# Search stage of a transformer block: the up weights' high parts copied right behind each Gelu, and the sums over gathered pairs moved apart from the next dots, with ScalarE's and GpSimd's orders changed to match

## The chip, the cores and the metric

The kernel runs on one core of a Trainium2 chip. The metric is the device time of one execution in microseconds (us). TensorE (PE) multiplies matrices, VectorE (DVE), ScalarE (ACT) and GpSimd (POOL) work on tiles, SyncE (SP) issues most of the transfers. Each engine runs its own instructions strictly in the order in which they were written; engines wait for each other by semaphores.

## The reference, cut to what matters

The whole reference is two transformer blocks over 512 tokens of width 1024. The change lies in the feed-forward part of the first block, a retrieval among 16384 single-neuron experts:

```python
q = einsum('bsd,de->bse', h, w_q).reshape(B, S, 8, 256)
s1 = einsum('bshd,hnd->bshn', q[..., :128], keys1)      # 128 keys a half
s2 = einsum('bshd,hnd->bshn', q[..., 128:], keys2)
v1, i1 = top_k(s1, 16); v2, i2 = top_k(s2, 16)
cand = v1[..., :, None] + v2[..., None, :]               # 256 candidates
vals, c = top_k(cand, 16)
expert = i1[c // 16] * 128 + i2[c % 16]
gate = softmax(vals)
u = u_tab[expert]; v = v_tab[expert]
out = einsum('te,ted->td', gate * gelu(einsum('td,ted->te', h, u)), v)
```

Three of the four blocks of 128 tokens are computed densely: all 16384 experts' `h . u` (the "up" products) go through the Gelu, are multiplied by a matrix of gates that is zero for experts that were not chosen, and then by all of `v_tab`. The fourth block of 128 tokens is computed by gathering: for each of its 128 chosen (head, rank) pairs a token's row of `u` and `v` is fetched by an indirect transfer.

## The kernel before, in words

**Stages.** The kernel is written out per engine, stage by stage, with no scheduler: the order in the source is the order of execution. The stage around the change is the search stage (`pe_route`, `act_route`, `dve_route`, `pool_route`, `sp_route`), about 946 to 1380 us in the profile. After it come the stage that builds the gates (`*_gates`, to about 1608 us) and the dense down stage (`*_experts`, to about 2300 us).

**Rounds.** The search stage has eight rounds, c = 0 to 7, one for each search head. In a round TensorE multiplies the queries of head c+1 (two halves f, 24 matmuls each with three passes for high and low parts), then eight up tiles n = 8c to 8c+7 (`pe_up`, 24 matmuls with 384 columns each), with the scores of head c+1 after the fourth (`pe_scores`). There are no queries and scores in round 7.

**Up tiles.** Tile n needs its weights in two parts. `sp_u` loads them to `ur` (three buffers), `act_u_hi` (L1629, ScalarE) copies the high part to `uhl`, `u_lo` (L1635, in this stage on GpSimd) subtracts it to get the low part, `pe_up` multiplies, and `act_up` (L1659) takes the Gelu out of the bank. `uhl` has three buffers, so the high part of tile n waits for the end of product n-3. Below, "hi(n)" and "lo(n)" are these two steps. The output banks form a ring of four.

**Search on VectorE.** `dve_top16` runs twice in a round: over the keys' scores ("key search", L1889 to L1901 with 128 columns), and over the 256 candidates ("candidate search", the same lines with 256). GpSimd builds the candidates (L1968) after the key search. Then follow the split of the indices (L1925 to L1928), two one-hot tiles (L1931) which GpSimd multiplies by the indices (L1980), and the subtraction of the maximum (L1932, step `gmax`). ScalarE takes the Exp (L1870, after a load of its function table, L1868), VectorE divides by the sum (L1937 to L1941), reduces the two GpSimd products (L1945) and writes the expert numbers (L1948 to L1952, the last is a cast to integers, step `idx`).

**Gathered pairs.** There are 64 pairs t, each of two gathers of 128 rows with 8 KB (u and v behind each other). In each round from the second on, three pairs pass. `pool_gather` (L1689) issues pair t; it waits for the sums of pair t-2, since `gs` has room for two pairs. `dve_dots` (L1700) multiplies the u halves with the tokens; `act_tick` (L1726) takes the Gelu; `dve_sums` (L1707, L1713) adds the v halves to the sum, which stands in a bank. A `dve_tick(t)` is `dve_dots(t)` followed by `dve_sums(t-1)`.

**Other engines.** GpSimd also splits the query weights (`split_lo`, L240, two a round). SyncE issues in a round the eight loads of `ur`, the stores of the Gelu's results, and the loads of query weights and keys; its load for tile n+5 stands behind the store of tile n and waits for lo(n+2).

Of the kernel before, what the change touches and what calls it, by code (L numbers as in the profile page):

```python
# [192 lines left out]
def build(nc, a):  # L193
# [1429 lines left out]
    def act_u_hi(e, n):  # L1623
        T, A, V, G = UP
        if n < P:
            e.wait_ge(*u_land[n % 3].of(n))
            if n >= 3:
                e.wait_ge(*T.of("up", n - 3))
            e.activation(uhl[n % 3][:, 0, :], ur[:, n % 3, :], ACT.Copy).then_inc(*A.up("hi", n))  # L1629
# [19 lines left out]

    def act_up(e, R, n):  # L1650
        T, A, V, G = UP
        act_u_hi(e, n + 2)
        to = ag[n % 3] if n < NE else agd[turn[n] % 3]
        if n >= NE:
            e.wait_ge(*DN[2].of("w", turn[n] - 3))
        elif n >= 3:
            e.wait_ge(*ag_saved[n % 3].of(n - 3))
        e.wait_ge(*T.of("up", n))
        e.activation(to[:, :], R.bank("up", n)[:, 0:DT], ACT.Gelu).then_inc(*R.out(A, "up", n))  # L1659

    def sp_up(e, n):
        T, A, V, G = UP
# [59 lines left out]
    def act_tick(e, t):  # L1722
        T, A, V, G = GA
        if t < NB:
            e.wait_ge(*V.of("dot", 2 * t + 1))
            e.activation(ga[:, 2 * t:2 * t + 2], dot[:, 2 * t:2 * t + 2], ACT.Gelu).then_inc(*A.up("ga", t))  # L1726
# [4 lines left out]
    R5 = Ring(banks[0:4], after=R4x)  # L1731
# [104 lines left out]
    def act_scores(e, c):  # L1836
        T, A, V, G = Q
        for half in range(2):
            e.wait_ge(*T.of("s", c, half))
            if c >= 2:  # L1840
                e.wait_ge(*V.of("k4", c - 2, 7))
            e.activation(SC[c % 2][:, 4 * half:4 * half + 4, :], in4(R5.bank("s", c, half)),
                         ACT.Copy).then_inc(*R5.out(A, "s", c, half))

    def act_route(e):
        T, A, V, G = Q
        all_done(e, *MG)
        split_hi(e, W2, 0)
        act_u_hi(e, 0)
        act_queries(e, 0)  # L1850
        split_hi(e, W2, 1)
        act_u_hi(e, 1)
        e.activation(sump, x1[:, 3, :], ACT.Copy).then_inc(*GA[1].up("out"))
        act_scores(e, 0)
        e.wait_ge(*V.of("h"))
        e.activation(h2r[:, :], h2p, ACT.Copy).then_inc(*GA[1].up("h"))
        for c in range(8):
            if c < 7:
                act_queries(e, c + 1)
                split_hi(e, W2, 2 * c + 2)  # L1860
                split_hi(e, W2, 2 * c + 3)
            act_up(e, R5, 8 * c)
            act_up(e, R5, 8 * c + 1)
            if c:
                act_tick(e, 3 * c - 3)
            act_up(e, R5, 8 * c + 2)
            act_up(e, R5, 8 * c + 3)
            e.preload_act_table_set(LN_SET)  # L1868
            e.wait_ge(*V.of("gmax", c))
            e.activation(e16[:, 2, :, c, :], e16[:, 2, :, c, :], ACT.Exp).then_inc(*A.up("gexp", c))  # L1870
            if c < 7:
                act_scores(e, c + 1)
            if c:
                act_tick(e, 3 * c - 2)
            act_up(e, R5, 8 * c + 4)
            act_up(e, R5, 8 * c + 5)
            if c:
                act_tick(e, 3 * c - 1)
            act_up(e, R5, 8 * c + 6)
            act_up(e, R5, 8 * c + 7)  # L1880
        for tb in range(3):
            e.wait_ge(*T.of("eT", tb))
            e.activation(eT[:, :, blk(tb)], R5.bank("eT", tb)[:, 0:3 * P].rearrange("p (a c) -> p a c", a=3),
                         ACT.Copy).then_inc(*R5.out(A, "eT", tb))
# [19 lines left out]
    def dve_route(e):  # L1904
        T, A, V, G = Q
        all_done(e, *MG)
        split_lo(e, W2, 0)
        split_lo(e, W2, 1)
        e.wait_ge(*h_land.of("h"))
        e.scalar_tensor_tensor(out=h2p, in0=x1[:, 3, :], scalar=small[:, 7:8], in1=h2r[:, :], op0=ALU.mult,  # L1910
                               op1=ALU.mult).then_inc(*V.up("h"))
        for c in range(8):
            k = c % 2
            e.wait_ge(*A.of("s", c, 1))
            dve_top16(e, V, 8, SC[k], S2, v16[k], i16[k], "k", c)
            if c:
                e.wait_ge(*G.of("oh", c - 1, 1))
            e.wait_ge(*V.of("k4", c, 7))
            e.tensor_copy(if16[:, :, :], i16[k][:, :, :]).then_inc(*V.up("if", c))
            if c:  # L1920
                dve_tick(e, 3 * c - 3)
            e.wait_ge(*G.of("cand", c))
            dve_top16(e, V, NT, cand, cand2, vv, ii, "c", c)
            e.wait_ge(*V.of("c4", c, NT - 1))
            e.tensor_scalar(cc[:, 0, :, :], ii[:, :, :], 4, None, ALU.logical_shift_right).then_inc(*V.up("hi", c))  # L1925
            e.tensor_scalar(cc[:, 1, :, :], ii[:, :, :], 15, None, ALU.bitwise_and).then_inc(*V.up("lo", c))
            e.wait_ge(*V.of("lo", c))
            e.tensor_copy(cf[:, :, :, :], cc[:, :, :, :]).then_inc(*V.up("cf", c))  # L1928
            e.wait_ge(*V.of("cf", c))
            for i in range(2):  # L1930
                e.tensor_tensor(oh4[i], by16(cf[:, i, :, :]), iota16, ALU.is_equal).then_inc(*V.up("oh", c, i))  # L1931
            e.tensor_tensor(e16[:, 2, :, c, :], vv[:, :, :], vv[:, :, 0:1].broadcast_to([P, NT, 16]),  # L1932
                            ALU.subtract).then_inc(*V.up("gmax", c))
            if c:
                dve_tick(e, 3 * c - 2)
            e.wait_ge(*A.of("gexp", c))
            e.tensor_reduce(sm4[:, :], e16[:, 2, :, c, :], AX.X, ALU.add).then_inc(*V.up("gsum", c))  # L1937
            e.wait_ge(*V.of("gsum", c))
            e.reciprocal(sm4[:, :], sm4[:, :]).then_inc(*V.up("ginv", c))
            e.wait_ge(*V.of("ginv", c))  # L1940
            e.tensor_tensor(e16[:, 2, :, c, :], e16[:, 2, :, c, :],  # L1941
                            sm4[:, :].unsqueeze(2).broadcast_to([P, NT, 16]), ALU.mult).then_inc(*V.up("gate", c))
            for i in range(2):
                e.wait_ge(*G.of("oh", c, i))
                e.tensor_reduce(e16[:, i, :, c, :], oh4[i], AX.X, ALU.add).then_inc(*(V.up("e", c) if i else V.up("e0", c)))  # L1945
            e.wait_ge(*V.of("e", c))
            s16 = slice(16 * c, 16 * c + 16)
            e.scalar_tensor_tensor(out=idxf[:, :], in0=e16[:, 0, 3, c, :], scalar=float(P), in1=e16[:, 1, 3, c, :],  # L1948
                                   op0=ALU.mult, op1=ALU.add).then_inc(*V.up("idxf", c))
            e.tensor_copy(gg16[:, s16], e16[:, 2, 3, c, :]).then_inc(*V.up("gg", c))  # L1950
            e.wait_ge(*V.of("gg", c))
            e.tensor_copy(idx[:, s16], idxf[:, :]).then_inc(*V.up("idx", c))  # L1952
            if c:
                dve_tick(e, 3 * c - 1)

    def pool_route(e):
        T, A, V, G = Q
        all_done(e, *MG)
        u_lo(e, 0)
        u_lo(e, 1)  # L1960
        for c in range(8):
            k = c % 2
            lo = lambda n: u_lo(e, 8 * c + n)
            lo(2)
            if c:
                e.wait_ge(*V.of("e0", c - 1))
            e.wait_ge(*V.of("k4", c, 7))
            e.tensor_tensor(cand.rearrange("p h (i j) -> p h i j", i=16), by16(v16[k][:, 0:4, :]),  # L1968
                            of16(v16[k][:, 4:8, :]), ALU.add).then_inc(*G.up("cand", c))
            if c < 7:  # L1970
                split_lo(e, W2, 2 * c + 2)
                split_lo(e, W2, 2 * c + 3)
            lo(3)
            if c >= 2:
                pool_gather(e, 3 * c - 2)
            lo(4)
            lo(5)
            for i in range(2):
                e.wait_ge(*V.of("oh", c, i))
                e.tensor_tensor(oh4[i], oh4[i], of16(if16[:, 4 * i:4 * i + 4, :]),  # L1980
                                ALU.mult).then_inc(*G.up("oh", c, i))
            lo(6)
            if c:
                pool_gather(e, 3 * c - 1)
            lo(7)
            lo(8)
            if c:
                pool_gather(e, 3 * c)
            else:
                pool_gather(e, 0)  # L1990
                pool_gather(e, 1)
            lo(9)
# [1283 lines left out]
```

## Time and profile before

| what | value |
|---|---|
| time, median of 3 runs | 3006.16 us (3005.68 to 3009.01) |
| the profiled execution's own time | 3007.56 us |
| its span | 3005.8 us |
| PE / DVE / ACT / POOL busy, share of the span | 93% / 66% / 38% / 18% |
| granted TensorE clock, mean | 0.97 |
| search stage | 946 to 1380 us |

The span is what the profiler sees from the first to the last instruction; the execution's own time is 1.8 us longer. Shares over the whole span hide that stages have different limits; the rows below look at single stages. A row of a timeline gives start, length, engine, line, operation, output and inputs, and in brackets how long the engine had been idle before it and what ended that. "x2" joins neighbours. A line is one of the kernel before, whose numbers the changed kernel moves by a few (L1659 becomes L1658, L1968 becomes L1975, L1980 becomes L1989, L1868 and L1870 become L1874 and L1876).

### The profile page before, as it was taken

To read this page: it belongs to the slowest core of one execution; us is meant where nothing else is said; L and a number is where in the kernel's file an instruction comes from. 1 tells how busy PE (TensorE), PEld (TensorE's weight loads), DVE (VectorE), ACT (ScalarE), POOL (GpSimd) and SP (SyncE) were. 2 spreads that over 40 slices of the span, in tenths; PEclk is the share of its full clock that TensorE was granted. 3 is DMA by queue.
4 is the path that set the end of the run, shared out by engine and by line. 5 is a ranking of instruction groups with operands and counts; after the bars stand their busy time and mean duration, and the time that the engine had idled before them with its cause. 6 is when DMAs were issued, how large, how long until landed. Compare 5 with 4: busy or idle time off the path is not lost.

```text
span 3005.8 us, 36696 instructions
## 1 busy us (share of the span) xinstructions
PE 2787.5 (93%) x14045; PEld 2364.5 (79%) x14045; DVE 1972.8 (66%) x3643; ACT 1140.9 (38%) x1678; POOL 543.3 (18%) x390
## 2 busy tenths in 40 slices
PE   8999999999998998988997999999997987899997
PEld 6787878887777888887996888888886556688876
DVE  3335665665555789899995887887886485444434
ACT  5445144223224333336884222222223444322222
POOL 0111221120002767663111111111110011000000
PEclk9999999999999999998998999999998999999999
DMA  4112100005552666576888788888882200222220
GB/s 155 50 50 98 57 29 29 29 29 196 210 203 86 227 243 249 215 265 238 323 311 319 283 302 308 292 292 293 292 291 86 79 29 2 98 92 98 96 98 28
DMA packets 141358, 501.17 MB, mean 167 GB/s; under 512 B 13401, under 2 KB 67073, under 8 KB 111617
## 3 DMA queue, kind: packets, MB, share of 16 engines
q1 hardware_dynamic: 122752, 364.60, 34.5%
q0 software_dynamic: 18432, 134.23, 11.3%
q8 instruction: 113, 1.85, 0.3%
q14 instruction: 61, 0.49, 0.1%
HBM read 450.53 MB, written 48.25 MB: 166 GB/s over the span
## 4 chain that ended last, share of the span: by engine, by line
PE 62%; DVE 23%; DMA 7%; ACT 4%; issue 3%; POOL 1%; SPq 0%; DVEq 0%; ACTq 0%; POOLq 0%
PE bank L244 16%; PE bank L245 16%; PE bank L246 16%; DMA gs<-in_uv_dram,idx 4%; DVE HA L2058 3%; DVE bank L1713 2%; DVE gs L1700 2%; DVE xn L1508 1%; PE bank L2658 1%; PE bank L1090 1%; PE bank L1080 1%; PE bank L713 1%; PE bank L1096 1%; DMA w_raw<-in_w_in_dram 1%; DVE uhl L1635 1%
## 5 line engine op out<-in xcount | busy, mean ns | idle before, releaser
L244 PE MATMUL bank<-HH,uhl 128*128 128x384 f32 x1024 | 358.3, 350 | 45.3 <-POOL uhl L1635 41.4
L245 PE MATMUL bank<-HL,uhl 128*128 128x384 f32 x1024 | 352.7, 344 | 0.0
L246 PE MATMUL bank<-HH,uhl 128*128 128x384 f32 x1024 | 352.3, 344 | 0.0
L244 PE MATMUL bank<-vhl,awhl 128*128 128x512 f32 x768 | 300.4, 391 | 6.8 <-DVE awhl L2291 6.8
L246 PE MATMUL bank<-vhl,awhl 128*128 128x512 f32 x768 | 300.3, 391 | 0.0
L245 PE MATMUL bank<-vhl,awhl 128*128 128x512 f32 x768 | 300.3, 391 | 0.0
L1689 POOL DMA_INDIRECT gs<-in_uv_dram,idx x128 | 161.2, 1259 | 753.6 <-DVE x L1713 497.0
L2242 ACT ACTIVATE vhl<-vraw 128x1024 fp32r<-128x1024 f32 x128 | 135.8, 1061 | 419.2 <-PE bank L246 253.4
L244 PEld LDWEIGHTS bank<-HH,uhl 128*128 128x128 f32 x1024 | 198.8, 194 | 52.6 <-issue 36.5
L1635 POOL TENSOR_TENSOR uhl<-ur,uhl 128x1024 fp32r<-128x1024 f32 x66 | 159.0, 2418 | 421.2 <-ACT uhl L1629 420.8
L2247 DVE TENSOR_TENSOR vhl<-vraw,vhl 128x1024 fp32r<-128x1024 f32 x128 | 156.5, 1223 | 104.0 <-ACT vhl L2242 103.9
L244 PE MATMUL bank<-HH,whl 128*128 128x512 f32 x528 | 217.3, 412 | 5.2 <-DVE whl L240 3.9
L240 DVE TENSOR_TENSOR whl<-w_raw,whl 128x2048 fp32r<-128x2048 f32 x49 | 113.5, 2316 | 161.5 <-ACT whl L234 161.5
L245 PE MATMUL bank<-HL,whl 128*128 128x512 f32 x528 | 210.7, 399 | 0.0
L246 PE MATMUL bank<-HH,whl 128*128 128x512 f32 x528 | 210.5, 399 | 0.0
L245 PEld LDWEIGHTS bank<-HL,uhl 128*128 128x128 f32 x1024 | 199.0, 194 | 1.7
L246 PEld LDWEIGHTS bank<-HH,uhl 128*128 128x128 f32 x1024 | 198.2, 194 | 0.0
L240 DVE TENSOR_TENSOR wfhl<-wf_raw,wfhl 128x2048 fp32r<-128x2048 f32 x37 | 84.8, 2292 | 155.4 <-ACT wfhl L234 155.4
L244 PEld LDWEIGHTS bank<-vhl,awhl 128*128 128x128 f32 x768 | 144.9, 189 | 36.6 <-DVE awhl L2291 4.4
L246 PEld LDWEIGHTS bank<-vhl,awhl 128*128 128x128 f32 x768 | 145.0, 189 | 30.4
L245 PEld LDWEIGHTS bank<-vhl,awhl 128*128 128x128 f32 x768 | 144.9, 189 | 29.1
L244 PE MATMUL bank<-HH,wfhl 128*128 128x512 f32 x352 | 139.6, 397 | 0.0
(420 smaller groups left out, 6233.6 us busy)
## 6 DMA issues: line engine op xcount, KB each, us to landing
ur<-in_peer_u_dram SPq DMA_DIRECT2D x128, 512.0 KB, 5.9
vraw<-in_peer_v_dram SPq DMA_DIRECT2D x128, 512.0 KB, 4.5
w_raw<-in_w_in_dram SPq DMA_DIRECT2D x36, 1024.0 KB, 4.9
xn<-in_ada_rows_dram SPq DMA_DIRECT2D x48, 512.0 KB, 4.7
g_scratch<-stg SPq DMA_DIRECT2D x12, 2048.0 KB, 11.0
gti<-g_scratch SPq DMA_DIRECT2D x16, 1536.0 KB, 10.0
wf_raw<-in_f_w_in_dram SPq DMA_DIRECT2D x22, 1024.0 KB, 4.8
act_scratch<-ag SPq DMA_DIRECT2D x96, 192.0 KB, 4.2
```

Of the source, the lines that this page charges most:

```text
L240: e.tensor_tensor(lo, W.tile(k), r32(hi), ALU.subtract).then_inc(*W.low(k).up(k))
L244: e.matmul(out, l[0], r[0], start=start, stop=False)
L245: e.matmul(out, l[0], r[1], start=False, stop=False)
L246: return e.matmul(out, l[1], r[0], start=False, stop=stop)
L713: i = e.matmul(b[:, (j - s) * P:wid[s]], const("tri_ge") if j == s else ones, L[:, off[j]:off[j] + wid[j]], start=j == s, stop=j == NT - 1 ...
L1635: e.tensor_tensor(uhl[n % 3][:, 1, :], ur[:, n % 3, :], r32(uhl[n % 3][:, 0, :]), ALU.subtract).then_inc(*u_low(n).up("lo", n))
L1689: e.indirect_dma_start(gs[:, n % 4, :], None, a["uv"], bass.IndirectOffsetOnAxis(ap=idx[:, n:n + 1], axis=0)).then_inc(*gs_land[n % 4].up(n))
L1700: e.scalar_tensor_tensor(out=u, in0=u, scalar=1.0, in1=h, op0=ALU.mult, op1=ALU.mult, accum_out=dot[:, n:n + 1]).then_inc(*V.up("dot", n))
L1713: e.scalar_tensor_tensor(out=x, in0=gs[:, n % 4, D:2 * D], scalar=ga[:, n:n + 1], in1=x, op0=ALU.mult, op1=ALU.add).then_inc(*(V.up("ax", ...
L2058: n = e.tensor_scalar(HA[k][:, i, :], iota, eT[:, 0, tok + i:tok + i + 1], eT[:, 2, tok + i:tok + i + 1], ALU.is_equal, ALU.mult)
L2242: e.activation(vhl[j % 3][:, 0, :], vraw[:, j % 2, :], ACT.Copy).then_inc(*A.up("v", j))
L2247: e.tensor_tensor(vhl[j % 3][:, 1, :], vraw[:, j % 2, :], r32(vhl[j % 3][:, 0, :]), ALU.subtract).then_inc(*V.up("v", j))
```

## The change

The number of instructions on each engine stays the same, and so does what they compute. Four things are written in another order.

1. `act_up(n)` issued hi(n+2) ahead of the Gelu of tile n; now it issues hi(n+3) behind it. As hi(n+2) used to follow the Gelu of n-1 with only the round's other work between them, the change is that this other work (queries, Exp, scores, ticks) now comes after the copy. It holds in the later stages too, which use the same function. hi(2) is issued once ahead of the loop.
2. VectorE's sums of a pair no longer stand right behind the next pair's dots: each stands halfway between its own pair's dots and the next.
3. ScalarE copies the scores of head c+1 before the Exp of round c, takes one more Gelu (tile 8c+4) before that Exp, and moves the third tick of a round behind its last Gelu.
4. GpSimd issues its gathers earlier or later to match, and splits its two one-hot products around a lo.

```diff
     def act_up(e, R, n):
         T, A, V, G = UP
-        act_u_hi(e, n + 2)
         to = ag[n % 3] if n < NE else agd[turn[n] % 3]
...
         e.activation(to[:, :], R.bank("up", n)[:, 0:DT], ACT.Gelu).then_inc(*R.out(A, "up", n))
+        act_u_hi(e, n + 3)
...
         for c in range(8):
+            if c > 1:
+                act_tick(e, 3 * c - 4)
             if c < 7:
                 act_queries(e, c + 1)
...
             act_up(e, R5, 8 * c + 2)
             act_up(e, R5, 8 * c + 3)
+            if c < 7:
+                act_scores(e, c + 1)
+            act_up(e, R5, 8 * c + 4)
             e.preload_act_table_set(LN_SET)
             e.wait_ge(*V.of("gmax", c))
             e.activation(e16[:, 2, :, c, :], e16[:, 2, :, c, :], ACT.Exp).then_inc(*A.up("gexp", c))
-            if c < 7:
-                act_scores(e, c + 1)
             if c:
                 act_tick(e, 3 * c - 2)
-            act_up(e, R5, 8 * c + 4)
-            act_up(e, R5, 8 * c + 5)
-            if c:
-                act_tick(e, 3 * c - 1)
-            act_up(e, R5, 8 * c + 6)
-            act_up(e, R5, 8 * c + 7)
+            for n in range(5, 8):
+                act_up(e, R5, 8 * c + n)
+        act_tick(e, 20)
...
             dve_top16(e, V, 8, SC[k], S2, v16[k], i16[k], "k", c)
+            if c > 1:
+                dve_sums(e, 3 * c - 4)
...
             if c:
-                dve_tick(e, 3 * c - 3)
+                dve_dots(e, 3 * c - 3)
             e.wait_ge(*G.of("cand", c))
             dve_top16(e, V, NT, cand, cand2, vv, ii, "c", c)
+            if c:
+                dve_sums(e, 3 * c - 3)
...
             if c:
-                dve_tick(e, 3 * c - 2)
+                dve_dots(e, 3 * c - 2)
             e.wait_ge(*A.of("gexp", c))
...
+            if c:
+                dve_sums(e, 3 * c - 2)
             for i in range(2):
                 e.wait_ge(*G.of("oh", c, i))
...
             if c:
-                dve_tick(e, 3 * c - 1)
+                dve_dots(e, 3 * c - 1)
```

GpSimd in round 3 before, from the candidates (L1968) on. `uhl` rows are lo steps, `wqhl` rows the split of the query weights, the `gs` rows a gathered pair each, and the two L1980 rows the one-hot products:

```order
L1968 TENSOR_TENSOR eT<-v_183 128x1024
L240 TENSOR_TENSOR wqhl_173<-wq_raw,wqhl_173 128x1024
L240 TENSOR_TENSOR wqhl_174<-wq_raw,wqhl_174 128x1024
L1635 TENSOR_TENSOR uhl_124<-ur,uhl_124 128x1024
L1689 DMA gs<-in_uv_dram,idx 128x2048 x2
L1635 TENSOR_TENSOR uhl_125<-ur,uhl_125 128x1024
L1635 TENSOR_TENSOR uhl_126<-ur,uhl_126 128x1024
L1980 TENSOR_TENSOR eT<-eT,if_186 128x1024
L1980 TENSOR_TENSOR oh<-oh,if_186 128x1024
L1635 TENSOR_TENSOR uhl_124<-ur,uhl_124 128x1024
L1689 DMA gs<-in_uv_dram,idx 128x2048 x2
L1635 TENSOR_TENSOR uhl_125<-ur,uhl_125 128x1024
```

And the same place now:

```order
L1975 TENSOR_TENSOR eT<-v_183 128x1024
L1689 DMA gs<-in_uv_dram,idx 128x2048 x2
L240 TENSOR_TENSOR wqhl_173<-wq_raw,wqhl_173 128x1024
L240 TENSOR_TENSOR wqhl_174<-wq_raw,wqhl_174 128x1024
L1635 TENSOR_TENSOR uhl_124<-ur,uhl_124 128x1024
L1635 TENSOR_TENSOR uhl_125<-ur,uhl_125 128x1024
L1689 DMA gs<-in_uv_dram,idx 128x2048 x2
L1635 TENSOR_TENSOR uhl_126<-ur,uhl_126 128x1024
L1989 TENSOR_TENSOR eT<-eT,if_186 128x1024
L1635 TENSOR_TENSOR uhl_124<-ur,uhl_124 128x1024
L1989 TENSOR_TENSOR oh<-oh,if_186 128x1024
L1635 TENSOR_TENSOR uhl_125<-ur,uhl_125 128x1024
```

The round's first gathered pair (3c-2) now stands ahead of the query weights' split and of lo(8c+3); the second (3c-1) stands ahead of lo(8c+5) instead of behind lo(8c+6); lo(8c+6) stands between the two one-hot products.

ScalarE in round 5 before, from the Gelu of tile 42 to the first tick after the Exp (`ag` rows are Gelus, `uhl` rows hi steps, `ga` rows ticks, `e` the Exp):

```order
L1659 ACTIVATE ag_128<-bank 128x384
L1629 ACTIVATE uhl_124<-ur 128x1024
L1659 ACTIVATE ag_129<-bank 128x384
L1868 ACT_TABLE_LOAD
L1870 ACTIVATE e_191<-e_191 128x4x16
L1842 ACTIVATE SC<-bank 128x512 x2
L1726 ACT_TABLE_LOAD
L1726 ACTIVATE ga<-dot 128x2
L1629 ACTIVATE uhl_125<-ur 128x1024
```

And the same place now, from the Gelu of tile 42:

```order
L1658 ACTIVATE ag_128<-bank 128x384
L1629 ACTIVATE uhl_124<-ur 128x1024
L1658 ACTIVATE ag_129<-bank 128x384
L1629 ACTIVATE uhl_125<-ur 128x1024
L1842 ACTIVATE SC<-bank 128x512 x2
L1658 ACTIVATE ag_130<-bank 128x384
L1629 ACTIVATE uhl_126<-ur 128x1024
L1874 ACT_TABLE_LOAD
L1876 ACTIVATE e_191<-e_191 128x4x16
L1726 ACT_TABLE_LOAD
L1726 ACTIVATE ga<-dot 128x2
```

Two hi steps, the copy of the scores and the Gelu of tile 44 (`ag_130`) moved ahead of the table load and the Exp.

VectorE at the start of round 4 before, from the last step of the key search to the candidate search:

```order
L1901 MAX_INDEX i_184<-v_182,S_181 128x8 x8
L1919 CAST if_186<-i_184 128x128
L1700 SCALAR_TENSOR_TENSOR gs,dot<-gs,bank 128x1024 x2
L1707 TENSOR_TENSOR ga<-ga,gg_156 128x2
L1713 SCALAR_TENSOR_TENSOR bank<-gs,ga,bank 128x1024 x2
L1889 MAX vv<-eT 128x8 x4
```

And now:

```order
L1902 MAX_INDEX i_184<-v_182,S_181 128x8 x8
L1707 TENSOR_TENSOR ga<-ga,gg_156 128x2
L1713 SCALAR_TENSOR_TENSOR bank<-gs,ga,bank 128x1024 x2
L1922 CAST if_186<-i_184 128x128
L1700 SCALAR_TENSOR_TENSOR gs,dot<-gs,bank 128x1024 x2
L1890 MAX vv<-eT 128x8 x4
```

The sums (L1707, L1713) of the pair before now stand ahead of the cast and of the next pair's dots; before, sums and dots stood side by side, dots first.

## Rows read from the trace of the kernel before

**Rows 1.** Busy time by stretch: length, PE, PEld, DVE, ACT, POOL busy, clock, DMA share, GB/s.

```profile
946.00:1380.00 434.00, 384.47 (x2021) 362.24 (x2019) 363.39 (x1040) 152.19 (x230) 286.89 (x145) 0.95 0.62 229
...
1700.00:2300.00 600.00, 600.00 (x2800) 517.53 (x2799) 471.92 (x688) 169.09 (x201) 72.97 (x54) 1.00 0.80 284
```

**Rows 2.** Waits in the search stage: total us, times, longest.

```profile
DVE gs L1700 <- DMA gs<-in_uv_dram,idx: 43.6, 21, 3.9
```

**Rows 3.** ScalarE's timeline, the Exp of rounds 1, 6 and 7: start us, length us.

```profile
1037.46 0.26 ACT L1870 ACTIVATE e<-e 128x64 f32<-128x64 f32 x1 [1.91 <-DVE e L1932]
...
1305.67 0.26 ACT L1870 ACTIVATE e<-e 128x64 f32<-128x64 f32 x1 [5.45 <-DVE e L1932]
...
1355.27 0.26 ACT L1870 ACTIVATE e<-e 128x64 f32<-128x64 f32 x1 [7.30 <-DVE e L1932]
```

**Rows 4.** ScalarE's timeline in rounds 3 and 4.

```profile
1172.10 0.60 ACT L1834 ACTIVATE pq<-bank 128x512 f32<-128x512 f32 x1 [5.00 <-PE bank L246]
...
1180.48 0.49 ACT L1659 ACTIVATE ag<-bank 128x384 f32<-128x384 f32 x1 [2.72 <-PE bank L246]
...
1184.64 0.49 ACT L1659 ACTIVATE ag<-bank 128x384 f32<-128x384 f32 x1 [2.63 <-PE bank L246]
1185.03 1.05 ACT L1629 ACTIVATE uhl<-ur 128x1024 fp32r<-128x1024 f32 x1
1193.21 0.49 ACT L1659 ACTIVATE ag<-bank 128x384 f32<-128x384 f32 x1 [7.13 <-PE bank L246]
1193.72 1.28 ACT L1868 ACT_TABLE_LOAD   x1
```

**Rows 5.** TensorE's timeline; then windows, columns as in Rows 1.

```profile
949.93 2.02 PE L1801 MATMUL bank<-keys,pq 128*128 128x128 f32 x16 [1.26 <-ACT pq L1834]
...
1187.12 0.41 PE L244 MATMUL bank<-HH,uhl 128*128 128x384 f32 x1 [2.58 <-POOL uhl L1635]
...
1347.87 0.41 PE L244 MATMUL bank<-HH,uhl 128*128 128x384 f32 x1 [1.78 <-POOL uhl L1635]
...
1190.00:1192.00 2.00, 2.00 (x8) 2.00 (x7) 2.00 (x11) 0.00 (x0) 2.00 (x2) 0.51 1.10 435
1348.00:1350.00 2.00, 2.00 (x12) 2.00 (x13) 1.97 (x10) 0.00 (x0) 2.00 (x1) 1.00 1.04 393
```

**Rows 6.** VectorE's timeline, rounds 5 and (one row) 6.

```profile
1220.19 1.64 DVE L1889 MAX8 v<-SC 128x8 f32<-128x128 f32 x8
...
1229.74 0.23 DVE L1919 CAST if<-i 128x128 f32<-128x128 uint32 x1
...
1237.36 1.40 DVE L1889 MAX8 vv<-eT 128x8 f32<-128x256 f32 x4
...
1244.84 4.20 DVE L1925 TENSOR_SCALAR cc<-ii 128x64 uint32<-128x64 uint32 x1
...
1251.72 2.42 DVE L1932 TENSOR_TENSOR e<-vv 128x64 f32<-128x64 f32 x1
...
1262.68 2.45 DVE L1948 SCALAR_TENSOR_TENSOR idxf<-e 128x16 f32<-128x16 f32 x1
...
1290.10 2.62 DVE L1713 SCALAR_TENSOR_TENSOR bank<-gs,ga,bank 128x1024 f32<-128x1024 f32 x2
```

**Rows 7.** GpSimd's timeline, round 5 and (last row) round 6.

```profile
1232.85 1.94 POOL L1968 TENSOR_TENSOR eT<-v 128x1024 f32<-128x1024 f32 x1
...
1239.45 2.39 POOL L1635 TENSOR_TENSOR uhl<-ur,uhl 128x1024 fp32r<-128x1024 f32 x1
...
1244.21 4.78 POOL L1635 TENSOR_TENSOR uhl<-ur,uhl 128x1024 fp32r<-128x1024 f32 x2
...
1293.48 0.95 POOL L1689 DMA_INDIRECT gs<-in_uv_dram,idx  x1 [3.44 <-DVE vv L1889]
```

**Rows 8.** ScalarE's timeline, end of the search stage.

```profile
1374.15 0.20 ACT L1726 ACTIVATE ga<-dot 128x2 f32<-128x2 f32 x1 [13.75 <-DVE gs L1700]
```

**Rows 9.** The page's DMA issues: KB each, median us from issue to landing.

```profile
ur<-in_peer_u_dram SPq DMA_DIRECT2D x128, 512.0 KB, 5.9
```

More of the change, by code:

```diff
@@ L1852, in act_route @@
         act_u_hi(e, 1)
+        act_u_hi(e, 2)
         e.activation(sump, x1[:, 3, :], ACT.Copy).then_inc(*GA[1].up("out"))
@@ L1969, in pool_route @@
                             of16(v16[k][:, 4:8, :]), ALU.add).then_inc(*G.up("cand", c))
+            if c >= 2:
+                pool_gather(e, 3 * c - 2)
             if c < 7:
@@ L1973, in pool_route @@
             lo(3)
-            if c >= 2:
-                pool_gather(e, 3 * c - 2)
             lo(4)
+            if c:
+                pool_gather(e, 3 * c - 1)
             lo(5)
@@ L1981, in pool_route @@
                                 ALU.mult).then_inc(*G.up("oh", c, i))
[L1982 to L1986, printed above, removed]
+                lo(6 + i)
             if c:
                 pool_gather(e, 3 * c)
-            else:
+            lo(8)
+            if not c:
                 pool_gather(e, 0)
```

## The prediction

> **What bounds the kernel now.** I read the busy time by stretch first. In the search stage TensorE is busy for 384 of 434 us, VectorE for 363, GpSimd for 287, at a mean clock of 0.95: none is full, so the stage is limited by engines that wait for each other in a ring. In the down stage TensorE is busy for all 600 us [rows 1]. Next come the waits of the search stage: VectorE's dots wait 21 times, 43.6 us in all, for gathered rows [rows 2], in rounds 1 to 7. To see the period of the ring I took one event that happens once a round, the Exp: from round 1 to round 6 it takes (1305.67 - 1037.46) / 5 = 53.64 us a round, from 6 to 7 49.60 us [rows 3].
>
> TensorE needs less than that. An up tile takes 1184.64 - 1180.48 = 4.16 us, half of the queries 5.00 + 0.60 = 5.60 us [rows 4], the scores 2.0 us [rows 5]: 8 x 4.16 + 2 x 5.60 + 2.0 = 46.5 us a round. The rest is waiting for lo steps, twice a round, and its after-effect: after a gap of 2.58 us at 1187.12 the granted clock is 0.51 (1.2 instead of 2.4 GHz), and that tile ends at 1193.2, 6.1 us after its start. After a gap of 1.78 us it stayed at 1.00 [rows 4, 5]. So there are three things to lose: VectorE's wait for the gathers, TensorE's gaps, and the slow clock behind them.
>
> **The gathers.** Before, pair t+1 can be issued once the sums of t-1 are done, and is needed one tick later. Now the sums of t-1 are done half a tick or more earlier. In a round the sums stand behind the key search, behind the candidate search and behind the division; the distance from there to the dots that need the new pair is always two or more long pieces of VectorE's work: key search 9.55, candidate search 7.48, sums 2.7 [rows 6]. Before, the waits were 2.1 us on average and 3.9 at most [rows 2]; sums that now stand one search, or the end of a round, earlier give more than that. I count VectorE's waits for gathers as gone.
>
> **The new ring.** I walk through one round with the end of the key search at 0. GpSimd: the first gather now stands ahead of the query weights' split and waits for sums that end at 2.7. The hand-over is 1293.48 - 1292.72 = 0.8 us [rows 6, 7], the pair itself 2.4 (1241.84 to 1244.21), the two splits 4.7 (1234.79 to 1239.45), lo(8c+3) 2.4 [rows 7]: it ends at 13.0. Before, this was 1.9 + 4.7 + 2.4 = 9.0, so TensorE's fourth tile gets its low part 4 us later than before, seen from the key search. Then 4.16 (tile 8c+3), 2.0 (scores), 4.16 (tile 8c+4), 0.4 (Gelu), 1.0 (hi) and 1.3 (table load) [rows 4, 5] bring ScalarE to the Exp; it is done at 26.4.
>
> VectorE does in that time: sums 2.7, cast 0.2, dots 2.3 (an estimate, a little under the sums), candidate search 7.5, sums 2.7, the split of the indices and the one-hots 2.9 (1251.72 - 1244.84, less a wait of 4.0 [rows 6]). Its maximum is subtracted at 18.4, or at 20.8 if L1932 waits for GpSimd as it did. So it now waits some 3 us for the Exp, which before waited for it. From the Exp to the next key search's end the work is that between L1932's end at 1254.14 and L1948's start at 1262.68, 8.5 us (the dots have changed sides, the sum is the same), then 0.5 for the three small steps, then 9.55 [rows 6]: 18.6. To it I add one full wait of 2.4 for the sums' first step and 0.4 for the division, see the next part: 21.4. The ring is 26.4 + 21.4 = 47.8 us, against TensorE's own 46.5 us. TensorE then waits 1.3 us a round at one place, short enough for its clock by the row above.
>
> **Waiting for GpSimd.** L1925 took 4.20 us at 1244.84 and ended at 1249.04, when GpSimd's two lo steps of 4.78 from 1244.21 ended at 1248.99. L1932 took 2.42 and L1948 2.45 [rows 6, 7]. Their own work is some 0.2 each, an estimate by the cast's 0.23, on larger tiles than two of them have. So some small VectorE steps stop until GpSimd's running instruction ends, and L1925 even until two had ended. GpSimd's work is 286.89 / 8 = 36 us a round [rows 1]. With hi earlier it does it nearly without a pause from the candidates on, so more of these steps meet it. What each pays lies between 0 and 2.4, and 7.2 if three lo steps stand in a row. On the ring are the division, the sums' first step and the index cast. I gave 1.2, 2.4 and 0. The cast should slip through, since it comes 2.6 us after the sums and the gather that waits for the same sums takes 0.8 + 2.4; that is a margin of 0.5. I therefore add a third of 2.4 to the period: 48.6 us.
> The Trainium skill (SBUF — State Buffer, "Who interferes with whom") says that VectorE and GpSimd share one port pair as an exclusive lock, that copies, casts and tensor_scalar can take it, and that the second to issue blocks fully. The trace agrees with its 4.20 against 0.23 us. Who gets the lock between two GpSimd instructions in a row is not said there.
>
> **The sum.** Exp of round 1: TensorE loses a gap of 2.6 in round 0, but tile 12, its Gelu and a hi now stand ahead of the Exp; I take 0.7 later. Rounds 1 to 6: 5 x (53.64 - 48.6) = 25.2 earlier. Round 7 has no queries, scores or split: from Exp to Exp it is 21.4 + 19.6 (the middle of 18.4 and 20.8) + 0.3 for the Exp + 0.8 for the third of a wait = 42.1 against 49.6, 7.5 earlier. The tail: before, ScalarE waited 13.75 us for the last dots and had the tick at 1374.15, 18.9 after the Exp, with two Gelus, two hi steps and three copies still to do [rows 3, 8]. Now two Gelus stand ahead of the tick, and GpSimd's lo(63) sets the last product: second gather from 15.5 to 18.7, then three lo steps and two one-hots of about 2.4 each to 30.7, the product to 34.9, which is 15 after the Exp at 19.9; 4 us earlier than the tick of before. In the gate stage hi used to be done while ScalarE waited for the product, and is now behind the Gelu: ScalarE is late by up to 1.0 [rows 4], once and not 27 times, as the next wait is shorter for it. I take 1.0 off. The down stage gives nothing: TensorE is full and stays so [rows 1]. Together -0.7 + 25.2 + 7.5 + 4.0 - 1.0 = 35.0 us. The profiled execution's own time was 3007.56, 1.8 more than its span and 1.4 more than the median; 3007.6 - 35.0 = 2972.6, as a median 2971 to 2973: **2972 us**.
>
> **Transfers.** The load of `ur` for tile 8c+6 is issued once lo(8c+3) is done at 13.0 and lands 5.9 us later [rows 9], at 18.9; ScalarE wants it at 17.6 and waits 1.3. That costs nothing: the next Gelu can't start before 23.2, and a hi and the scores' copies take 2.1. The cover is gone when the landing takes over 8 us; each us beyond it goes into the ring. Behind ScalarE's waiting hi stand the next scores and the Exp, for which VectorE waits.
>
> **The rivals.**
> A (0.50), the forecast: periods of 47.8 to 50, 2967 to 2980 us.
> B (0.15), TensorE alone: VectorE's steps slip between GpSimd's, the period is 46.5. Five rounds bring 35.7, the rest 12: 2960. For it speaks that nothing else in the walk is over 46.5 by more than 1.3.
> C (0.24), one more wait for GpSimd, or landings of 8 us and more, on the ring: 50.2. Then TensorE's gap is 3.7 us, over the 2.58 that halved the clock, and its next tile takes 6.1 instead of 4.16, which is on the ring as well: 52.1. Five rounds bring 7.7, the rest 9: 2991.
> D (0.06), slower: the index cast (L1952) comes too late by 0.5 us and stands behind lo(8c+8), lo(8c+9) and lo(8c+10), as L1925 stood behind two. 47.8 + 7.2 + 1.9 = 56.9 a round, 16 us lost in five, some 5 won elsewhere: 3018. It decides when the wait is over 6 us a round, thus from the third lo on. Against it stands only the margin of 0.5 us. By the Trainium skill's rule above, a cast is of the kind that can be blocked.
> E (0.05), the change doesn't do what it says: GpSimd reaches its gathers no earlier, the period stays near 55 and the ends' gain is used up: 3006.
>
> **The numbers.** From B's 2960 to C's 2991 lie all but 0.11; with a margin for the walk 2958 to 2993. A measurement of this kernel tells 0.2%, 6 us, from no change. Faster by more: A, B, C and a part of E, 0.90. Within: 0.04. Slower: 0.06.
>
> **What would show it.** In the profile after: VectorE's waits for `gs` in the search stage below 8 us; TensorE's waits for lo steps below 15 us, and its clock near 1.00; VectorE now waiting for the Exp about 3 us a round; Exp to Exp 48 to 49 us in rounds 1 to 6. Longer lengths of L1707, of the division or of the index cast, and the gap ahead of tile 8c+3, would show C or D. The prediction is wrong if the period is over 51, which would be a wait on the ring that I left out or made too small: most likely at a small VectorE step beside GpSimd, or at ScalarE ahead of the Exp.

## The result and the profile after

The changed kernel takes 3023.54 us (median of 4 runs, 3021.95 to 3024.95), the kernel before 3005.92 us (4 runs, 3004.95 to 3009.01): a ratio of 1.006, with a 95% interval of 1.0048 to 1.0072. It is slower by 0.6%, little but clear of the noise, where 2972 us was forecast. The time lies outside the 2958 to 2993 us that were given; rival D, 3018 us at a chance of 0.06, comes nearest.

First the Exp once a round, from ScalarE's timeline of the changed kernel, rounds 1, 2, 3, 6 and 7, to be set against [rows 3]:

```profile
1033.96 0.26 ACT L1876 ACTIVATE e<-e 128x64 f32<-128x64 f32 x1
...
1092.85 0.26 ACT L1876 ACTIVATE e<-e 128x64 f32<-128x64 f32 x1
...
1150.97 0.26 ACT L1876 ACTIVATE e<-e 128x64 f32<-128x64 f32 x1
...
1321.69 0.26 ACT L1876 ACTIVATE e<-e 128x64 f32<-128x64 f32 x1
...
1374.76 0.26 ACT L1876 ACTIVATE e<-e 128x64 f32<-128x64 f32 x1
```

From round 1 to 6 that is (1321.69 - 1033.96) / 5 = 57.55 us a round (58.1 from round 2 to 3) against 53.64 before. The Exp of round 1 comes 3.5 us earlier, the one of round 7 comes 19.5 later. The wait in brackets behind before's rows is gone: the Exp no longer waits for VectorE. The prediction called itself wrong for a period over 51 us, and named a small VectorE step beside GpSimd as the likeliest cause.

The waits of the search stage of the changed kernel (total us, times, longest):

```profile
ACT ag L1658 <- PE bank L246: 182.4, 50, 13.3
...
PE bank L244 <- POOL uhl L1635: 59.0, 13, 9.5
...
DVE sm L1942 <- ACT e L1876: 39.0, 8, 6.0
...
ACT uhl L1629 <- DMA ur<-in_peer_u_dram: 10.6, 7, 3.2
```

VectorE's wait for gathered rows, 43.6 us before [rows 2], is in the list no more. VectorE waits for the Exp instead, about 5 us each time. TensorE waits 59.0 us for lo steps, up to 9.5 us at a time; before it was 41.4 us and at most 5.1.

VectorE is busier by 20 us, from the busy time by stretch (columns as in [rows 1]), though no operation was added:

```profile
946.00:1380.00 434.00, 374.67 (x1968) 354.69 (x1967) 383.40 (x1022) 148.70 (x219) 278.17 (x141) 0.93 0.63 224
```

Its groups of the search stage, with the line, the tile, the count, then busy us and mean ns of one, say where:

```profile
L1957 DVE COPY gg<-e 128x16 f32<-128x16 f32 x8 | 52.5, 6564 | 0.0
...
L1946 DVE TENSOR_TENSOR e<-e,sm 128x64 f32<-128x64 f32 x8 | 38.0, 4750 | 0.3
...
L1955 DVE SCALAR_TENSOR_TENSOR idxf<-e 128x16 f32<-128x16 f32 x8 | 2.6, 326 | 0.3
...
L1959 DVE CAST idx<-idxf 128x16 uint32<-128x16 f32 x8 | 1.4, 175 | 0.3
```

A copy of 128x16 numbers takes 6.6 us in the mean, and the division 4.8. Before, the copy took 161 ns and the division 940. Three other small steps had waits before and have lost most of them: the split of the indices (L1925, now L1930) went from 2404 to 420 ns, the subtraction of the maximum (L1932, now L1937) from 2417 to 494, and L1948 (now L1955) from 2162 to 326. The waits for GpSimd did not only grow, they moved to other steps. To see what the copy waits for, VectorE's timeline of the changed kernel in round 2, from the end of the Exp's wait on:

```profile
1093.14 0.22 DVE L1942 TENSOR_REDUCE sm<-e 128x4 f32<-128x64 f32 x1 [5.98 <-ACT e L1876]
...
1093.61 4.07 DVE L1946 TENSOR_TENSOR e<-e,sm 128x64 f32<-128x64 f32 x1
1097.60 0.15 DVE L1707 TENSOR_TENSOR ga<-ga,gg 128x2 f32<-128x2 f32 x1
1097.78 2.62 DVE L1713 SCALAR_TENSOR_TENSOR bank<-gs,ga,bank 128x1024 f32<-128x1024 f32 x2
...
1102.68 0.17 DVE L1955 SCALAR_TENSOR_TENSOR idxf<-e 128x16 f32<-128x16 f32 x1
1102.77 7.84 DVE L1957 COPY gg<-e 128x16 f32<-128x16 f32 x1
1110.64 0.17 DVE L1959 CAST idx<-idxf 128x16 uint32<-128x16 f32 x1
```

and GpSimd's timeline beside it:

```profile
1092.82 2.39 POOL L1989 TENSOR_TENSOR oh<-oh,if 128x1024 f32<-128x1024 f32 x1
1095.18 2.41 POOL L1635 TENSOR_TENSOR uhl<-ur,uhl 128x1024 fp32r<-128x1024 f32 x1
1101.17 0.97 POOL L1689 DMA_INDIRECT gs<-in_uv_dram,idx  x1 [3.58 <-DVE bank L1713]
1102.45 0.94 POOL L1689 DMA_INDIRECT gs<-in_uv_dram,idx  x1 [0.30 <-issue]
1103.41 7.16 POOL L1635 TENSOR_TENSOR uhl<-ur,uhl 128x1024 fp32r<-128x1024 f32 x3
1122.61 1.93 POOL L1975 TENSOR_TENSOR eT<-v 128x1024 f32<-128x1024 f32 x1 [12.03 <-DVE i L1902]
...
1128.15 4.65 POOL L240 TENSOR_TENSOR wqhl<-wq_raw,wqhl 128x1024 fp32r<-128x1024 f32 x2
1132.76 4.68 POOL L1635 TENSOR_TENSOR uhl<-ur,uhl 128x1024 fp32r<-128x1024 f32 x2
```

The copy ends at 1110.61, GpSimd's three lo steps end at 1110.57: it waits through lo(8c+8), lo(8c+9) and lo(8c+10), and past the two boundaries between them. The division ends at 1097.68, GpSimd's run of a one-hot and a lo step at 1097.59. Then GpSimd itself stands 12.03 us, until the key search that was late by the same copy is done: the three lo steps were done early, and the fourth tile's has to wait for the next candidates and splits. TensorE pays for that. Its timeline, and then the window at the start of that tile (columns as in [rows 1]):

```profile
1135.24 0.66 PE L244 MATMUL bank<-HH,uhl 128*128 128x384 f32 x1 [9.08 <-POOL uhl L1635]
```

```profile
1135.50:1137.50 2.00, 2.00 (x7) 2.00 (x7) 1.97 (x1) 0.00 (x0) 1.95 (x1) 0.50 0.65 123
```

After a gap of 9.08 us the granted clock is 0.50, that is 1.2 instead of 2.4 GHz, and the Gelu comes 7.0 us after the tile's start (1142.27), not 4.16.

### The profile page after: what moved, and what is told of

Same layout as the page of the kernel before. It is cut to its first block, busy times and chain, and to the rows that moved or that the text cites. A ratio compares the mean times of both kernels' runs of the same rounds, so it can differ in the third digit from the quotient of the medians.

```text
span 3022.5 us, 36696 instructions
## 1 busy us (share of the span) xinstructions
PE 2781.8 (92%) x14045; PEld 2361.9 (78%) x14045; DVE 2009.3 (66%) x3643; ACT 1143.1 (38%) x1678; POOL 541.4 (18%) x390
## 4 chain that ended last, share of the span: by engine, by line
PE 39%; DVE 10%; ACT 2%; DMA 1%; issue 1%; POOL 0%; SPq 0%; DVEq 0%; ACTq 0%; POOLq 0%
PE bank L244 12%; PE bank L246 12%; PE bank L245 12%; DVE HA L2064 2%; PE bank L2664 1%; DVE uhl L1635 1%; DVE HO L2061 1%; DVE M L2870 1%; DVE bank L1713 1%; DVE m L2866 1%; DVE gs L1700 1%; DMA vraw<-in_peer_v_dram 1%; ACT stg L2110 1%; PE bank L2590 1%; DVE M L2859 0%
## 5 line engine op out<-in xcount | busy, mean ns | idle before, releaser
L1629 ACT ACTIVATE uhl<-ur 128x1024 fp32r<-128x1024 f32 x128 | 134.5, 1052 | 20.0 <-DMA ur<-in_peer_u_dram 20.0
```

## The experiments

The theory: the loss is the copy (with the division in second place) held behind GpSimd's uninterrupted run, the rest of the walk is right. The rivals: the Exp behind tile 8c+4, so that VectorE waits for it; the earlier high parts; GpSimd's order of gathers. All ratios are to the kernel before on the same chip (its medians there are 3003.06, 3005.82 and 3007.62 us); "period" is Exp to Exp from round 1 to 6, divided by 5.

**One wait more on GpSimd.** lo(8c+8) waits until the index cast is done, so that GpSimd pauses for the small steps.

```diff
                 pool_gather(e, 3 * c)
+            e.wait_ge(*V.of("idx", c))
             lo(8)
```

> The changed kernel with one wait more: GpSimd waits for the index cast of the round before it starts lo(8c+8). Theory 1 (a small VectorE copy that finds GpSimd busy is kept out until a whole run of GpSimd instructions ends, and this is what made the round 58.2 us long): the copy L1957 shrinks from 7.85 to about 0.2 us, the Exp-to-Exp period falls by the 7.7 us and by the slow clock behind TensorE's 9 us gap, to 48 to 51 us, the time to 2965 to 2980 us. Rival 2 (the late first gather and lo(8c+3) set the round, the copy only fills time that would be waited anyway): the copy shrinks, but the period stays within 2 us of 58, the time 3010 to 3024 us. Rival 3 (the copy's length is not due to GpSimd): it stays at 7.8 us.

Measured: 2973.76 us, ratio 0.9897 (0.988 to 0.9914), period 49.9. The groups of VectorE and its timeline, then GpSimd's; the copy starts as far behind the second gather's start as above, 0.33 us (0.32 there):

```profile
L1946 DVE TENSOR_TENSOR e<-e,sm 128x64 f32<-128x64 f32 x8 | 45.1, 5631 | 0.3
...
L1957 DVE COPY gg<-e 128x16 f32<-128x16 f32 x8 | 1.3, 168 | 0.0
```

```profile
1145.90 0.17 DVE L1957 COPY gg<-e 128x16 f32<-128x16 f32 x1
1146.10 0.41 DVE L1959 CAST idx<-idxf 128x16 uint32<-128x16 f32 x1
```

```profile
1145.57 0.94 POOL L1689 DMA_INDIRECT gs<-in_uv_dram,idx  x1 [0.31 <-issue]
1146.59 7.20 POOL L1635 TENSOR_TENSOR uhl<-ur,uhl 128x1024 fp32r<-128x1024 f32 x3
```

The gather alone does not hold the copy: it took 0.17 us while the gather ran. What held it for 7.84 us was that lo(8c+8) stood ready behind the gather. With one wait the kernel is some 50 us faster than the changed one, and nearly as fast as forecast. The whole order of gathers and the Exp's place are still those of the change, so neither is what made it slow.

**Without the copy.** The sums read the gates where they lie (an edit of L1707, not printed here), and one copy at the end of the stage takes the place of the eight.

```diff
-            e.tensor_copy(gg16[:, s16], e16[:, 2, 3, c, :]).then_inc(*V.up("gg", c))
-            e.wait_ge(*V.of("gg", c))
+            e.wait_ge(*V.of("idxf", c))
             e.tensor_copy(idx[:, s16], idxf[:, :]).then_inc(*V.up("idx", c))
```

> The changed kernel without the copy of the gates in each round (the sums of this stage read them where they stand; one copy at the stage's end). Theory 1: the index cast behind it starts at the same place, finds the gather and the run of three lo steps, and takes over the 7.8 us; the period stays within 1 us of 58.2 and the time within 4 us of the changed kernel's 3023. Rival (it is this copy, its form or its operands, that is slow): the round loses 7.7 us and more, 2965 to 2980 us.

Measured: 3019.36 us, ratio 1.0054 (1.0037 to 1.0071), period 57.3. From VectorE's groups:

```profile
L1959 DVE CAST idx<-idxf 128x16 uint32<-128x16 f32 x8 | 51.7, 6468 | 0.3
```

The cast inherits the wait. What counts is the place, not which small step stands there.

**The length of the run.** The same wait, one lo step later, leaves a run of one.

```diff
             lo(8)
...
+            e.wait_ge(*V.of("idx", c))
             lo(9)
```

> The changed kernel with GpSimd's wait for the index cast one lo step later than in x1_wait_idx: ahead of lo(8c+9), so that exactly one lo step follows the gather without a pause. Theory (a small copy waits until a run of GpSimd instructions ends, so its length is that of the run): the copy takes 7.85 less the two lo steps that now come behind the pause, some 3.1 us; the period is 50.5 + 3 = 53 to 55 us, the time 2985 to 2997 us. Rival 1 (the copy waits for the running instruction alone and loses the rest elsewhere): 7.8 us and 3020 us as in the changed kernel. Rival 2 (the gather's own descriptors block it, not the lo steps): below 1 us and 2974 us.

Measured: 2994.96 us, ratio 0.9957 (0.994 to 0.9973), period 52.2. The time is as expected, the period some 1 us below the expected one. In most rounds the copy slips through and the cast behind it waits: the cast now takes 2206 ns in the mean and the copy 532. VectorE's timeline in round 3 has

```profile
1154.39 2.91 DVE L1959 CAST idx<-idxf 128x16 uint32<-128x16 f32 x1
```

which ends at 1157.30; GpSimd's lo(8c+8) starts at 1154.84 and takes some 2.4 us. So a small step behind the gather pays what remains of the run: 7.8 us with three lo steps, 2.9 with one, nothing with none.

**The two parts alone.** The high parts behind the Gelu are put alone on the kernel before (the first lines of the change's diff, and the prelude's hi(2)). Then they alone are taken back from the changed kernel, so that the new orders remain:

```diff
         T, A, V, G = UP
+        act_u_hi(e, n + 2)
...
         e.activation(to[:, :], R.bank("up", n)[:, 0:DT], ACT.Gelu).then_inc(*R.out(A, "up", n))
-        act_u_hi(e, n + 3)
```

> The kernel before with the first part of the change alone: hi(n+3) behind the Gelu instead of hi(n+2) ahead of it, all orders else as before. Theory 1: earlier hi steps let GpSimd's lo steps follow each other without a pause, so the small VectorE steps behind the reductions (L1948, L1950, L1952) meet a run of lo steps and take 5 to 8 us a round where they took 2.8; the gathers' waits partly hide it: 3000 to 3020 us. Rival (the fault lies only in the new orders; hi alone removes TensorE's gaps of 2.4 us behind the Exp): 2990 to 3003 us, small VectorE steps as before.

> The changed kernel with hi(n+2) ahead of the Gelu of n, as before, and all the new orders. Theory 1: hi(8c+10) is then copied only behind the third tick and the queries of the next round, so GpSimd's run behind the gather is one lo step shorter (lo(8c+8), lo(8c+9)); the copy L1957 takes some 5.4 instead of 7.8 us, the period is about 55 to 56, the time 3008 to 3016 us. Rival (the hi part is harmless and what made the round long is the orders alone): within 3 us of 3023.

Measured: the high parts alone 2982.53 us, ratio 0.9929 (0.9912 to 0.9946), period 50.7; the orders alone 3018.73 us, ratio 1.0053 (1.0037 to 1.007), period 54.7. I had expected little of the first, and missed. The orders alone lie between the two ranges that were given for them (3008 to 3016, and within 3 us of 3023). The first is the useful half as it stands, though its VectorE too meets GpSimd in a run:

```profile
L1949 DVE SCALAR_TENSOR_TENSOR idxf<-e 128x16 f32<-128x16 f32 x8 | 32.1, 4010 | 0.3
```

In the orders alone the copy takes 4107 ns in the mean (5.4 us were expected) and the division 6132. The slow-down comes with the new orders, the longer copy (6564) with both together.

**High parts alone with a wait of their own**, on lo(8c+7), the first of the two lo steps that L1949 waits through there:

```diff
+            e.wait_ge(*V.of("idx", c))
             lo(7)
```

> x2_hi_only (the kernel before with the hi steps behind the Gelu) with one pause in GpSimd's run: a wait for the index cast ahead of lo(8c+7). All other orders are as before, dots and sums side by side too. Theory (the pause is what matters, the new order of the sums is worth what VectorE's waits for gathers are in x2, 21.3 us, of which lo(8c+7) gives some back): L1949 shrinks from 4.0 to 1 to 2.4 us, the time is 2965 to 2980 us. Rival (the new orders do the work in x6_exp_and_gate): no better than x2, 2981 to 2990 us.

Measured: 2984.68 us, ratio 0.9927 (0.991 to 0.9943), period 50.7, no better than without it, as the rival of that run had it. L1949 now takes 176 ns, but in the waits of the search stage stands:

```profile
DVE gs L1700 <- DMA gs<-in_uv_dram,idx: 50.1, 15, 7.9
```

In the high parts alone this wait was 21.3 us. The 28.8 us more are about what L1949 lost, 8 times 3.8 us: the gathers' wait takes the small step's place. So with the old places of the sums this cure is worth nothing; with the new ones it is worth some 50 us. The new orders do what the prediction said of gathers.

**The division.** Three kernels on top of the first wait: the Exp back ahead of tile 8c+4's Gelu; a second wait, the second one-hot behind the division; both.

```diff
-            act_up(e, R5, 8 * c + 4)
             e.preload_act_table_set(LN_SET)
...
-            for n in range(5, 8):
+            for n in range(4, 8):
                 act_up(e, R5, 8 * c + n)
...
             for i in range(2):
-                e.wait_ge(*V.of("oh", c, i))
+                e.wait_ge(*(V.of("gate", c) if i else V.of("oh", c, 0)))
```

> x1_wait_idx (GpSimd waits for the index cast ahead of lo(8c+8)) with the Exp back ahead of the Gelu of tile 8c+4; the scores' copy still stands ahead of it. In x1 the period is 50.7 us and VectorE waits 4.9 us a round for the Exp. Theory: the ring loses that wait, and the division then starts earlier against GpSimd's run of one-hots and lo steps, where it waits for the run's end (up to 7 us instead of 5.1), so only 1 to 3 us a round are won: 2955 to 2970 us. Rival (the Exp's place is not on the ring any more): 2971 to 2976 us.

> x1_wait_idx with GpSimd's wait for the division ahead of the second one-hot alone, Exp behind the Gelu of 8c+4 as in the change. Theory: the division shrinks from 5.1 to 2.5 us or less, and 2 to 4 us of the 50.7 us round go: 2952 to 2966 us. Rival (GpSimd's pause costs TensorE as much): 2970 to 2978 us.

> x5_exp_first, and GpSimd also waits for the division ahead of its second one-hot product, so that the division finds a pause. Theory (the division L1946 waits for the end of GpSimd's whole run): it shrinks from 5 to 7 us to at most 2.5, the sums behind it start at once, the period comes to TensorE's own 46.5 to 48 us: 2945 to 2960 us. Rival (GpSimd is so loaded that a pause in it makes lo(8c+6) and lo(8c+7) late for TensorE): the division shrinks, TensorE waits 2 to 4 us a round for lo instead, the time is that of x5 or above.

Measured: the Exp's place alone 2973.95 us, ratio 0.9894 (0.9878 to 0.9911); the wait alone 2955.07, 0.9836 (0.982 to 0.9852), period 47.7; both 2949.85, 0.9816 (0.9799 to 0.9832), period 46.7. In the first of them I had expected 1 to 3 us a round and got none: 2973.95 us lies in the range of that run's rival (2971 to 2976). VectorE waits no more for the Exp (0.7 us in all), but the division takes what was won, as VectorE's timeline and GpSimd's say:

```profile
1131.26 10.14 DVE L1945 TENSOR_TENSOR e<-e,sm 128x64 f32<-128x64 f32 x1
```

```profile
1129.43 2.42 POOL L1635 TENSOR_TENSOR uhl<-ur,uhl 128x1024 fp32r<-128x1024 f32 x1
...
1138.90 2.42 POOL L1635 TENSOR_TENSOR uhl<-ur,uhl 128x1024 fp32r<-128x1024 f32 x1
```

The division came 1.8 us into a run of five instructions that ends at 1141.32, and ended at 1141.40, past four boundaries. With GpSimd's second wait alone the division's mean is 942 ns. With both edits it is 4521 ns still, where at most 2.5 us were expected: the division now starts as a one-hot product does (1123.14 and 1123.15 us in round 3), and waits through that and the lo step behind it, up to GpSimd's pause. The time came as expected all the same. With the division so shortened, the Exp's place is worth 5 us (2955.07 against 2949.85). TensorE is then near full, 420 of 434 us in the busy time by stretch of the kernel with both:

```profile
946.00:1380.00 434.00, 420.00 (x2370) 400.77 (x2369) 406.95 (x1175) 202.08 (x313) 299.69 (x152) 0.98 0.73 264
```

In rounds 1 to 5 (1029 to 1262 us) it is busy for 232 of 233 us, and its 46.7 us a round is the 46.5 that the prediction gave TensorE alone. This version beats the kernel before by 56 us.

**One gather back in its old place**, behind lo(8c+3), on top of the first wait, so that the low part of the fourth tile comes earlier:

```diff
-            if c >= 2:
-                pool_gather(e, 3 * c - 2)
...
             lo(3)
+            if c >= 2:
+                pool_gather(e, 3 * c - 2)
```

> x1_wait_idx with the round's first gathered pair back behind lo(8c+3), which undoes that part of GpSimd's new order. By my walk lo(8c+3) comes 3 to 4 us earlier against the key search; if it is on the ring, the period falls from 50.7 to 47 to 48 us and TensorE's gap of 1.9 us goes: 2955 to 2965 us. Rival (the gather then comes too late for its dots, whose distance shrinks by some 8 us): VectorE waits for gathered rows again and the time stays at 2970 or rises.

Measured: 2970.36 us, ratio 0.9885 (0.9868 to 0.9901), period 49.2. The interval overlaps that of the first wait alone. Neither expectation came true: the period fell by 0.7 us and not by 3, and no wait for gathered rows came back. The division takes 6664 ns in the mean, against 5631 with the first wait alone, and the cast of the key indices (L1922) 1862 against 800, so part of what the earlier lo step gave went into these two. What the gather's place is worth without them was not measured; as a cause of the slow-down it was ruled out by the first wait, which left it in its new place.

## Why the prediction was wrong

The prediction's step that failed is "Waiting for GpSimd": "I gave 1.2, 2.4 and 0. The cast should slip through, since it comes 2.6 us after the sums and the gather that waits for the same sums takes 0.8 + 2.4; that is a margin of 0.5."

**The margin was there and did not help.** The sums ended at 1100.40, the gathers ran from 1101.17 to 1103.39, and the copy (the step ahead of the cast) started at 1102.77, 0.64 us ahead of the lo step. It stood all the same until the run's end. A start ahead of GpSimd's next instruction, as the profile draws it, is not enough when that instruction is ready behind a gather. The condition of rival D ("comes too late by 0.5 us") was thus wrong too, its price for the step right: 7.2 us were named, 7.7 measured. That D's time is near is in part luck: its period has 2.4 us for the sums' first step, which paid nothing, and only 0.4 for the division, which paid 3.9.

**The price per step was the wrong kind of number.** I priced a step at one GpSimd instruction, and took the 4.20 us of L1925 [rows 6] across two of them [rows 7] for an exception. In the changed kernel, from round 1 on, it was the rule in all the long ones: the copy waits across the boundaries between three lo steps, the division across one to three. It is not the rule everywhere. In the kernel before, L1932 of [rows 6] (1251.72, 2.42 us) ended at 1254.14, when the first of two one-hot products had ended, though the second followed at once, as GpSimd's timeline of the kernel before shows:

```profile
1250.74 3.32 POOL L1980 TENSOR_TENSOR eT<-eT,if 128x1024 f32<-128x1024 f32 x1 [1.76 <-DVE eT L1931]
1254.02 2.41 POOL L1980 TENSOR_TENSOR oh<-oh,if 128x1024 f32<-128x1024 f32 x1
```

So the price to plan with is up to the rest of GpSimd's run. The Trainium skill (SBUF — State Buffer, "Who interferes with whom") says that whoever issues first gets the shared port pair for its whole instruction, and that the other is blocked for as long. The copy's 7.84 us agrees that a step can be blocked. But by the profile the copy started ahead of the three lo steps and was blocked through all of them, while the gather that was running did not hold it in the run with one wait; for this the measurement decides. That the ports are what the copy waits for is the page's account; the runs here show only when it waits and for how long.

**The period.** From key search to Exp's end: 26.4 forecast, 28.8 measured (1122.4 to 1151.2). TensorE's tile behind lo(8c+3) started 12.8 us after the key search, 13.0 forecast; the 2.4 more come with the tile behind the 9.08 us gap at half clock (7.0 instead of 4.16). From the Exp's end to the key search's end: 21.4 forecast, 29.3 measured. In it the division pays 3.9 and the copy 7.7; the sums' first step, given 2.4, pays nothing (0.15 us in all), the division had been given 0.4, and the rest was 0.9 too long (0.7 of this was the division's wait of the kernel before, 0.88 us long at 1259.51, inside the 8.5 us taken from there): 21.4 + 3.9 + 7.7 - 2.4 - 0.4 - 0.9 = 29.3. Together 58.1.

**The other terms** of the sum, forecast and measured: the Exp of round 1 0.7 later, 3.5 earlier; five rounds 25.2 earlier, 19.5 later; round 7 7.5 earlier, 3.5 later (1374.76 - 1321.69 = 53.07 against 49.60 [rows 3]). The tail was to be 4 earlier and is 0.5 later, from two timelines of VectorE, the changed kernel's and then the kernel before's, at the gate stage's first step:

```profile
1398.20 0.36 DVE L2126 TENSOR_SCALAR ne<-eT 128x384 f32<-128x384 f32 x1 [1.47 <-issue]
```

```profile
1378.23 0.36 DVE L2120 TENSOR_SCALAR ne<-eT 128x384 f32<-128x384 f32 x1 [1.39 <-ACT eT L1883]
```

There the division took 8.28 us and the copy 5.37. Behind this point, where 1.0 was to be lost, 3.3 came back; which step gave it was not followed. 3.5 - 19.5 - 3.5 - 0.5 + 3.3 = -16.7, the difference of the spans (3022.5 and 3005.8).

**What was right.** The gathers' wait is gone. TensorE's own 46.5 us holds in the best version. The landing of `ur` costs ScalarE 10.6 us in all, 3.2 at most; behind most of these waits the next Gelu still waits for TensorE. VectorE waits for the Exp, 5 us rather than 3. With the one failed step taken out, by one wait, the time is 2973.76 us against the 2972 forecast; part of that closeness is luck, since its period is 49.9 and not 48.6 (the division's mean is 5.6 us). That is 6.7 us in five rounds, of which the earlier Exp of round 1 (1033.95, so 3.5 earlier and not 0.7 later) makes up 4.2.

## What to carry to other kernels

When a small step of VectorE stands on the ring, price it by up to the rest of GpSimd's back-to-back run, not by one instruction, and treat a margin of a few tenths of a us in its favour as none. Where a change fills GpSimd's pauses, look for the small steps that used those pauses. A wait that makes GpSimd stand for 0.2 us of VectorE's work can be worth several us a round; each such step needs its own, since a cured one hands its gain to the next.

## What was not expected of the hardware

- A 128x16 copy takes 0.17 us while a gather is running and nothing is ready behind it, and 7.84 us at the same distance from the gather's start when three lo steps are ready behind it.
- A 128x64 division crossed up to four boundaries between GpSimd's instructions (10.14 us). But a 128x64 subtraction in the kernel before (L1932, 2.42 us) got in at the first boundary of two one-hot products. What decides who gets in between two instructions was not found.
- TensorE's clock: in the kernel with the first wait, a gap of 1.89 us at 1170.85 was followed by a granted clock of 0.50 over the 3.2 us from 1171.4 on, where the gap of 1.78 us before had 1.00 behind it [rows 5]. The prediction's "short enough for its clock" thus holds for little more than the row it was read from. That window, columns as in [rows 1]:

```profile
1171.40:1174.60 3.20, 3.20 (x12) 3.20 (x11) 3.13 (x3) 0.00 (x0) 1.66 (x1) 0.50 0.88 248
```
